# Mixture-of-experts weights in another slot order, with whole transfers and rows spread by a repeated column

## The reference

```python
def _hier_moe(h, w_group, b_group, w_expert, b_expert, w_gate, w_up, w_down):
    ...                                   # top-1 group, top-2 of its 8 experts, combine weights
    for g in range(N_GROUPS):             # 4 groups of 8 experts
        a = jnp.einsum('td,edf->tef', t, w_gate[g])
        u = jnp.einsum('td,edf->tef', t, w_up[g])
        act = jax.nn.silu(a) * u * combine[:, g, :, None]
        y = y + jnp.einsum('tef,efd->td', act, w_down[g])

def reference(x, p, ...):
    for i in range(DEPTH):                # 2
        x = x + mixer(_rmsnorm(x, norm_mix[i]), ...)
        x = x + _hier_moe(_rmsnorm(x, norm_ffn[i]), ...)
        gate = jax.nn.sigmoid(_rmsnorm(x, norm_ple[i]) @ ple_w_gate[i])
        x = x + gate * (p[i] @ ple_w_proj[i])
    return x
```

## Time and profile before

| | us |
|---|---|
| median of 3 executions | 842.86 (839.48, 842.86, 842.89) |
| the profiled execution's own time | 839.04 |
| its span, first to last instruction | 837.3 |
| PE busy | 750.0 (90%) |
| DVE, ACT, POOL busy | 377.8, 229.5, 189.8 |
| HBM read | 241.07 MB |

### The profile page before, as it was taken

The page is one execution under the profiler, slowest core; times in us unless marked ns, Lnnn a source line. Parts: engine busy times, 40 slices in busy tenths (PEclk is TensorE's granted clock), DMA queues, the critical chain, the costliest instruction groups (busy, mean ns, idle before and its releaser), DMA issues.

```text
span 837.3 us, 10837 instructions
## 1 busy us (share of the span) xinstructions
PE 750.0 (90%) x4121; PEld 413.0 (49%) x4121; DVE 377.8 (45%) x672; ACT 229.5 (27%) x416; POOL 189.8 (23%) x206
## 2 busy tenths in 40 slices
PE   2677879899999999889999977898999999989897
PEld 1555844643334333334778866456343343433366
DVE  6996842532222232213776968225332233222264
ACT  3323121431111110103675537143001111110163
POOL 5874420321111011000426560012210111100000
PEclk8598979999999999999999999999999999999999
DMA  7036061799999999999489572582899999999861
GB/s 227 1 58 203 2 237 70 282 413 412 412 413 413 412 416 411 413 415 370 175 253 280 206 287 66 205 286 113 306 412 413 412 413 413 412 416 411 344 228 50
DMA packets 79636, 244.48 MB, mean 292 GB/s; under 512 B 22080, under 2 KB 23120, under 8 KB 71008
## 3 DMA queue, kind: packets, MB, share of 16 engines
q1 hardware_dynamic: 75392, 240.24, 74.6%
q0 software_dynamic: 1408, 3.24, 1.8%
q10 hardware_dynamic: 2784, 0.30, 0.3%
HBM read 241.07 MB, written 1.64 MB: 290 GB/s over the span
## 4 chain that ended last, share of the span: by engine, by line
PE 81%; DVE 7%; issue 5%; ACT 3%; DMA 1%; POOL 1%; SPq 1%; ACTq 0%; DVEq 0%
PE PS L1833 27%; PE PS L1863 13%; PE PS L1579 11%; PE PS L1873 7%; PE PS L2053 3%; PE PS L1761 3%; PE PS L1703 2%; PE PS L1637 2%; PE PS L1802 2%; PE PS L1957 2%; PE PS L1844 1%; POOL qrs L717 1%; PE PS L1718 1%; ACT prob L1000 1%; PE PS L1663 1%
## 5 line engine op out<-in xcount | busy, mean ns | idle before, releaser
L1833 PE MATMUL PS<-ring,xe 128*64 128x512 f32 x1024 | 228.0, 594 | 17.4 <-issue 15.0
L1833 PEld LDWEIGHTS PS<-ring,xe 128*64 128x64 f32 x1024 | 76.9, 137 | 163.6 <-issue 163.6
L1863 PE MATMUL PS<-ring,actT 128*64 128x512 f32 x512 | 116.9, 598 | 1.7 <-DVE actT L1341 1.4
L632 POOL COPY xe<-xg 128x512 f32 x60 | 47.6, 793 | 296.8 <-PE PS L1833 276.3
L1355 DVE TENSOR_TENSOR olo<-PS,ohi 128x512 fp32r<-128x512 f32 x64 | 44.2, 691 | 123.3 <-ACT ohi L892 123.3
L1341 DVE COPY actT<-PS 128x256 f32<-128x256 f32 x32 | 13.6, 424 | 173.1 <-PE PS L1844 173.1
L892 ACT ACTIVATE ohi<-PS 128x512 fp32r<-128x512 f32 x64 | 38.2, 597 | 153.1 <-PE PS L1863 153.1
L1046 DVE SCALAR_TENSOR_TENSOR ringr<-ring,gT,dwh 128x512 fp32r<-128x512 f32 x80 | 63.6, 846 | 25.9 <-ACT dwh L763 24.6
L884 ACT ACTIVATE act<-PS 128x256 f32<-128x256 f32 x32 | 12.3, 383 | 223.8 <-PE PS L1833 223.8
L1863 PEld LDWEIGHTS PS<-ring,actT 128*64 128x64 f32 x512 | 34.7, 136 | 67.2 <-issue 67.2
L1579 PE MATMUL PS<-ringr,rawh 128*128 128x512 f32 x160 | 63.4, 396 | 0.8 <-DVE ringr L1046 0.8
(11 more groups left out here) (321 smaller groups left out, 970.6 us busy)
## 6 DMA issues: line engine op xcount, KB each, us to landing
ring<-in_moe_w_gate SPq DMA_DIRECT2D x128, 512.0 KB, 16.5
ring<-in_moe_w_up SPq DMA_DIRECT2D x128, 512.0 KB, 17.3
ring<-in_moe_w_down SPq DMA_DIRECT2D x64, 1024.0 KB, 17.4
ring<-in_nat_w_qkv SPq DMA_DIRECT2D x6, 2048.0 KB
ring<-in_ple_w_gate SPq DMA_DIRECT2D x4, 2048.0 KB
ring<-in_s_w_out SPq DMA_DIRECT2D x2, 2048.0 KB
ring<-in_nat_w_o SPq DMA_DIRECT2D x2, 2048.0 KB
ring<-in_s_w_in SPq DMA_DIRECT2D x1, 2048.0 KB
```

Source lines behind the costliest of these rows:

```text
L632: pool.tensor_copy(xe[:, e % 4, :, :], xg[:, :, bass.ds(first, CAP)]).then_inc(S("xe_ready"), 1)
L1833: ins = mm(PS[CAP * h_:CAP * h_ + CAP, 0, :].rearrange("p (u f) -> p u f", u=2), xe[:, (2 * p + h_) % 4, k, :], wv[h_][:, k], start=k == 0 ...
L1863: ins = mm(PS[CAP * h_:CAP * h_ + CAP, 2 + n, :], actT[:, k, CAP * h_:CAP * h_ + CAP], wd[h_][:, k, 512 * n:512 * n + 512], start=k == 0, ...
```

## The change

**Slots.** In layer 0 experts 2 and 3 of each six now have slots 4 and 5, experts 4 and 5 slots 0 and 1. `ys`, `yT[4]` and `glu` of the mixer moved out of slots 4 and 5, and the wait on `x_ready` is gone, so four experts' loads stand behind `y_done` where two did. The PLE's three items of layer 0 moved from slots 0, 1, 2 to 2, 3, 0. QKV, W_o and layer 1 are turned by two slots, which keeps what each of them waits for.

**Transfers.** The first six experts and pairs 5 to 15 ask for gate and up whole, 8 KB a partition, after `gu_done` alone; only pairs 3 and 4 come in halves. Where a pair came whole, PE waits for all of it before its first half.

**Rows.** `diag`, `rows` and `spread_rows` are gone. `spread_row` takes the column `slot` (or `wgt`) repeated 128 times as the stationary operand, against the identity: 4 matmuls of 128x128 each. The slots' row comes ahead of `gather`, the weights' row after its fourth k. `sel` is made and used one token half at a time for k = 0 and 1. POOL no longer waits for `row_done`. `wrow` is copied out when `gather` is through.

**Last combine.** `combine` of pair 15 stands ahead of the wait for `pj`, where it stood behind.

```diff
-        moe_items(0, (2, 3, 0, 1, 4, 5))
-        IT["ple"] = [ple_items(0, 0)]
+        moe_items(0, (2, 3, 4, 5, 0, 1))
+        IT["ple"] = [ple_items(0, 2)]
...
-        moe_items(1, (3, 0, 4, 5, 1, 2))
-        IT["ple"].append(ple_items(1, 1))
+        moe_items(1, (1, 2, 4, 5, 3, 0))
+        IT["ple"].append(ple_items(1, 3))
...
+        IN_HALVES = (3, 4)
+
+        def in_halves(n):
+
+            return (n - moe_item[0 if n < moe_item[1] else 1]) // 2 in IN_HALVES
...
-                for half, sem in enumerate((loaded[s], later[s])):
-                    cs = slice(1024 * half, 1024 * half + 1024)
-                    sp.dma_start(ring[s][:, 0:2048][:, cs], gate_[1][:, cs]).then_inc(sem, 16 if half else 64)
-                    sp.dma_start(ring[s][:, 2048:4096][:, cs], up_[1][:, cs]).then_inc(sem, 16)
+                sp.dma_start(ring[s][:, 0:2048], gate_[1]).then_inc(loaded[s], 80)
+                sp.dma_start(ring[s][:, 2048:4096], up_[1]).then_inc(later[s], 32)
...
+                if not in_halves(n):
+                    sp.wait_ge(S("gu_done"), NP * i + e // 2 - 2)
+                    for m in (n, n + 1):
+                        s, (gate_, up_, down_) = items[m]
+                        sp.dma_start(ring[s][:, 0:2048], gate_[1]).then_inc(loaded[s], 80)
+                        sp.dma_start(ring[s][:, 2048:4096], up_[1]).then_inc(later[s], 32)
+                    return
...
+            def gather_part(i, k, t):
+                for w, half in enumerate((hhi, hlo)):
+                    ins = mm(PS[:, GBANK[k], :], half[:, t, k, :], sel[:, t, :], start=(w, t) == (0, 0),
+                             stop=(w, t) == (1, 1))
+                return ins
...
+            def spread_row(i, n, what):
+
+                for j in range(2):
                     for t in range(TT):
-                        ins = mm(PS[:, GBANK[k], :], half[:, t, k, :], sel[:, t, :], start=(w, t) == (0, 0),
-                                 stop=(w, t) == (1, 1))
-                ins.then_inc(S("gather_done"), 1)
-
-            def spread_rows(i):
-
-                for n in range(2):
-                    pe.wait_ge(S("xg_ready"), KD * i + n + 3)
-                    pe.wait_ge(S("diag_ready"), 2 * TT * i + TT * n + TT)
-                    mm(PS[:, 2 + n, :], ones[:, :].bitcast(F32), diag[:, n].rearrange("p j t s -> p (j t s)"), start=True, stop=True)\
-                        .then_inc(S("row_done"), 1)
+                        ins = mm(PS[:, 4 + n, T * j + P * t:T * j + P * t + P], bc(what[:, t, j], 1, P), ident[:, :],
+                                 start=True, stop=True)
+                ins.then_inc(S("row_done"), 1)
...
                     if k0 == 0:
                         arrived(pe, it)
-                    else:
+                    if k0 or not in_halves(it):
                         later_arrived(pe, it)
...
                 down(i, NP - 1, 0)
                 down(i, NP - 1, 1)
+                combine(i, NP - 1)
                 pj = IT["ple"][i][1]
...
-                combine(i, NP - 1)
```

More of the change, by code:

```diff
@@ L194, in ple_items @@
             return (a, b, c)
-        moe_items(0, (2, 3, 0, 1, 4, 5))
-        IT["ple"] = [ple_items(0, 0)]
+        moe_items(0, (2, 3, 4, 5, 0, 1))
+        IT["ple"] = [ple_items(0, 2)]
         wq = I["nat_w_qkv"][0].rearrange("(k p) n -> p k n", p=P)
-        IT["qkv"] = [item((3 + n) % 4, (0, wq[:, :, 512 * n:512 * n + 512])) for n in range(6)]
+        IT["qkv"] = [item((1 + n) % 4, (0, wq[:, :, 512 * n:512 * n + 512])) for n in range(6)]
         wo = I["nat_w_o"][0].rearrange("(k p) n -> p k n", p=P)
-        IT["wo"] = [item((1 + n) % 4, (0, wo[:, :, 512 * n:512 * n + 512])) for n in range(2)]
-        moe_items(1, (3, 0, 4, 5, 1, 2))
-        IT["ple"].append(ple_items(1, 1))
+        IT["wo"] = [item((3 + n) % 4, (0, wo[:, :, 512 * n:512 * n + 512])) for n in range(2)]
+        moe_items(1, (1, 2, 4, 5, 3, 0))
+        IT["ple"].append(ple_items(1, 3))
         prev, nth, last, cnt = [], [], {}, {}
@@ L297, in program @@
               enumerate((A_R + 16384, A_R + 20480, A_O, A_O + 4096, A_H + 12288, O1 + 20480))]
-        ys = at("ys", [P, L, 8, SH], F32, A_XG + 24576)
-        yT = [at(f"yT{n}", [P, SW // P, T], F32, A_XG + 4096 * n) for n in range(5)]
-        glu = [at(f"glu{n}", [P, 512], F32, A_XG + 20480 + 2048 * n) for n in range(2)]
+        ys = at("ys", [P, L, 8, SH], F32, A_H + 8192)
+        yT = [at(f"yT{n}", [P, SW // P, T], F32, A_H + 4096 if n == 4 else A_XG + 4096 * n) for n in range(5)]
+        glu = [at(f"glu{n}", [P, 512], F32, A_O + 2048 * n) for n in range(2)]
         RX = A_W
@@ L519, in _ @@
                 for e in range(6):
-                    if items[m0 + e][0] == 4:
-                        if i == 0:
-                            sp.wait_ge(S("x_ready"), 1)
-                        else:
-                            sp.wait_ge(S("pv_done"), NPR)
+                    if i == 1 and items[m0 + e][0] == 4:
+                        sp.wait_ge(S("pv_done"), NPR)
                     load_gate_up(m0 + e)
@@ L1272, in route @@
                         bc(PS[:, 4, 0:TT * NE].rearrange("p (t e) -> p t e", t=TT), 2, 2), ALU.mult))
-                link(ve.tensor_reduce(slot[:, :, :].rearrange("p t j -> p (t j)"),
-                                      ptmp[:, :, :, :].rearrange("p t j e -> p (t j) e"), AX.X, ALU.add))
+                ve.tensor_reduce(slot[:, :, :].rearrange("p t j -> p (t j)"),
+                                 ptmp[:, :, :, :].rearrange("p t j e -> p (t j) e"), AX.X, ALU.add)\
+                    .then_inc(S("route_steps"), 1)
+                ve.wait_ge(S("route_steps"), 3 * i + 1)
                 ve.wait_ge(S("wr_ready"), 2 * i + 2)
                 for t in range(TT):
-                    ins = ts(sel[:, t, :], iota_s[:, :], slot[:, t, 0:1], None, ALU.is_equal)
-                link(ins)
-                for t in range(TT):
+                    link(ts(sel[:, t, :], iota_s[:, :], slot[:, t, 0:1], None, ALU.is_equal))
                     stt(sel[:, t, :], iota_s[:, :], slot[:, t, 1:2], sel[:, t, :].bitcast(F32), ALU.is_equal,
@@ L1300, in bounds_of, with weights_row @@
                 link(ts(col[:, :], col[:, :], -1.0, None, ALU.add))
[L1302 to L1308, removed]
+            def weights_row(i):
                 ve.wait_ge(S("gex_ready"), i + 1)
@@ L1311, in rows @@
                 link(ve.reciprocal(wgt[:, :, 0], den[:, :]))
[L1312 to L1315, removed]
+                tt(wgt[:, :, 1], e21[:, :], wgt[:, :, 0], ALU.mult).then_inc(S("route_steps"), 1)
             def rows_evict(i):
@@ L1361, in moe @@
                 route(i)
+                weights_row(i)
                 bounds_of(i)
-                rows(i)
                 rows_evict(i)
@@ L1884, in moe @@
                 places(i)
-                constant(5)
+                constant(4)
+                pe.wait_ge(S("route_steps"), 3 * i + 1)
+                spread_row(i, 0, slot)
                 pe.wait_ge(S("hhi_ready"), TT * (i + 1))
                 pe.wait_ge(S("hlo_ready"), TT * (i + 1))
-                pe.wait_ge(S("sel_ready"), TT * (i + 1))
                 pe.wait_ge(x_part[i], 4)
-                for k in range(KD):
+                for t in range(TT):
+                    pe.wait_ge(S("sel_ready"), TT * i + t + 1)
+                    for k in range(2):
+                        ins = gather_part(i, k, t)
+                        if t:
+                            ins.then_inc(S("gather_done"), 1)
+                for k in range(2, KD):
                     gather(i, k)
+                    if k == 3:
+                        pe.wait_ge(S("route_steps"), 3 * i + 2)
+                        pe.wait_ge(S("route_steps"), 3 * i + 3)
+                        spread_row(i, 1, wgt)
                 for p in range(NP):
                     gate_up(i, p, 0, 4)
-                    if p == 0:
-                        spread_rows(i)
                     gate_up(i, p, 4, KD)
```

13 lines of the change are left out of this document (7 added, 6 removed).

## The result

| | us |
|---|---|
| kernel before, median of 12 in this comparison | 840.52 (835.41 to 842.89) |
| changed kernel, median of 12 | 843.81 (841.86 to 849.00) |
| ratio, 95% interval | 1.0056 [1.0035, 1.0078] |
| profiled execution, before and after | 839.04, 843.37 |
| its span | 837.3, 841.6 |

By the ratio the change makes the kernel slower by 0.56%, 4.7 us, just past the half per cent that can be told; the interval begins at 0.35%, and the two medians lie 3.3 us apart. The prediction had 843.0 with 834 to 849 around it, and called that no change against a median before of 842.86.

A forecast was written before the change was run, and what follows sets the result against it. Landing of pair 15's gate and up was taken to bound each layer's experts, then PE from dense_mm. Layer 0 +4.4 and layer 1 -1.5 gave +2.9 on 839.0, 841.9; the median was put at 843.0 us, range 834 to 849.

The forecast's parts named there:

- The forecast of no change: Whole kernel: a median of 843.0 against 842.86 before; chance 0.48 of staying within 0.5%, 4.2 us.
- Early loads, -1.7: Layer 0's stream: four experts loaded early bring pair 15's second half from 374.6 to 372.9 us, -1.7; nothing in layer 1.
- Rows, end of pair 0: Both layers: pair 0 ends 2.2 us sooner and starts 0.2 sooner; the stream gains 2.0 of 2.9, -2.2 a layer.
- Whole transfers, -3.5 and +3.4: Pairs 5 to 15, both layers: 422 instead of 409 GB/s, -3.5; pair 15 takes 7.04 us after its last byte, +3.4.
- Clock falls, +0.8 before pair 15: PE in both layers: a fall to 1.2 GHz costs 1.7 us, half counted; layer 1's gather gains 0.8.
- Last down product in layer 0: 387.2 forecast: End of pair 15's down product in layer 0: 387.2 us instead of 390.4, 3.2 earlier.
- The late PLE weights, 18.6 us behind it: PLE of layer 0: pj waits for pair 15, dense_mm starts 18.6 us behind the down product against 11.0, +7.6.
- Layer 1's combine, +0.8: Layer 1's PLE: the last combine runs ahead of the transposes and copy of p, +0.8 us.
- The stream wins: Rival: whole transfers at 430 GB/s, thin queue cured, no clock falls; -7.1 us, 834 to 836; chance 0.27.
- PE in the cold at the PLE: Rival: low clock at layer 0's PLE and pair 15s, thin queue uncured; +11.2 at worst, likely 849 us; chance 0.25.
- The early loads do nothing: Rival: something else holds layer 0's stream, so the 1.7 us are missing; 844.7 us; chance 0.05.
- three things that would have made me wrong: Signs against the forecast: ga landing before 396, the stream exceeding 425 GB/s, or PE waiting for pairs 5 to 10.

The follow-up runs named there:

- experiment 8: The kernel before with the early loads of layer 0 alone; 841.69 us, 1.0007 to the kernel before.
- experiment 2: The kernel before with only the dense blocks' slots turned as in the change, so PLE weights wait for pair 15; 847.24 us, 1.0094.
- experiment 10: The changed kernel with 8 constant matmuls between the halves of pair 0 in both layers; 847.25 us, 1.0097 to the kernel before.
- experiment 7: The kernel before with the new rows and selection alone; 838.10 us, 0.9976 to the kernel before.
- experiments 3: The changed kernel with every pair from 3 to 15 in halves; 843.15 us, 1.0041 to the kernel before.
- experiment 4: The changed kernel with pair 15 in halves besides 3 and 4; 841.33 us, 1.0022 to the kernel before.
- experiments 1: The changed kernel with the dense blocks' old slots, so PLE weights wait for pair 14; 838.68 us, 0.9983 to the kernel before.
- experiment 9: The changed kernel with PLE weights behind pair 14, pairs 11 to 15 also in halves, last combine behind the transposes of p; 830.72 us, 0.9885.
- experiment 12: The version of experiment 9 with pairs 3 and 4 whole too; 833.42 us, 0.9920 to the kernel before.

## Why the prediction was right in sum and wrong in a step

**The forecast of no change.** Measured +0.56%. The sum, +2.9 on 839.04, was near; the 1.1 us that took 841.9 to 843.0 were added because the three executions of the kernel before had a median of 842.86. Over twelve executions that median is 840.52, so as a difference the forecast said +0.1 where +3.3 was measured by the medians and 4.7 by the ratio. That 843.0 lies so near 843.81 is in part luck.

**Early loads, -1.7.** Right in mechanism and size, -1.6 by the trace of experiment 8; no median shows it alone. It gave layer 0's gather, with the same idle gap as layer 1's, no price for the clock that it lost in experiments 2 and 8.

**Rows, end of pair 0.** PE's part came: pair 0 to pair 1 is 2.08 us shorter, by 2.2 in the step, and each row's 4 matmuls take 1.05 us for 1.0. What failed is "With pair 0 and pair 1 over 2.2 us sooner I take 2.0 of the 2.9". By experiment 10 it is 1.0 to 1.25 in a layer, by experiment 7 1.3 in layer 1 and nothing in layer 0. I had read the thin stretch in layer 1's window and applied it to layer 0, where the queue was still full at pair 0's end; it becomes thin there only through the early loads, so the two parts pay together: from pair 0's start to pair 15's second half the early loads save 1.6 us without the new rows and 3.3 with them (200.22 in experiment 7, 196.95 in 3, whose first six experts come whole too). The change itself shows the stretch still thin, 303 GB/s from 593 to 603. "There the queue is nearly empty" was not a reading either: the DMA engines were busy for 0.98 of the stretch at 354 GB/s, and are for 0.92 here. Why they move less while busy is open. Pair 3's 4.19 MB, 10 us of data, are asked for at 591.27 and 594.71, and pair 4's first half follows at 599.52.

**Whole transfers, -3.5 and +3.4.** Measured -2.9 by landing (experiments 3 and the change) and +3.4; the rate went from 413 to 421, not 422. A layer is 0.5 worse for it by the traces, and all halves were 0.7 us better in all, by medians that can't be told apart. The Trainium skill (DMA: Bandwidth & Descriptors, Anatomy of one DMA) has 2.0 us of fixed cost in a transfer; its fit is for single transfers issued by GpSimd, and these are issued by SP into a full queue. Here 44 fewer transfers a layer, with rows twice as long, gave 2.9 us in all, 0.07 each, so that cost is not paid for each transfer in this queue, as the prediction had said.

**Clock falls, +0.8 before pair 15.** The place was wrong. The fall came at pair 14 in both layers, and the wait for pair 15's data covered all of it. It counts as soon as the data are early, as experiment 4 shows. In layer 1 the gather gained 1.5 us, where I took 0.8 with 0.2 of the start.

**Last down product in layer 0: 387.2 forecast, 388.7 measured.** Against `glu_done`, which was itself 0.9 later, the forecast is 0.6 off: the data 1.4 later than its -7.4 (a thin queue worth less, whole transfers worth less), the clock 0.8 better.

**The late PLE weights, 18.6 us behind it.** Measured 17.3: p lands 5.9 us after its issue (7.0 by the earlier trace rows), `ga` 11.2 (12.4), and the low clock costs 5.33 - 3.70 = 1.6 where I took 1.7. `dense_mm` was forecast at 405.8 and starts at 406.00. This step carried the forecast, and experiments 1 and 2 bear it out.

**Layer 1's combine, +0.8.** Measured +0.8 (from the last down product's end to `dense_mm` 11.3 before, 12.1 after), 1.1 by experiment 9.

**The sum.** Layer 0 +4.4 forecast, +3.7 measured; layer 1 -1.5 and -0.7. The other 1.3 us lie in the two mixers, which the sum doesn't touch. Of the 0.9 before `glu_done`, the clock from 125 to 150 was 0.97 instead of 1.00. It was 0.94 to 1.00 in the runs with early loads and 0.97 in experiment 2, which has none and reached `glu_done` at 151.61, so the early loads need have no part in it. By its traces the change costs +3.0 where the sum said +2.9; errors of a microsecond went both ways in it.

**The rivals.** "The stream wins" fell with 421 GB/s, under the 430 from which it decides. "PE in the cold at the PLE" came in one part, the low clock at the projections; at 17.3 us it stayed under its 20. "The early loads do nothing" has the median of experiment 8 for it and the trace, -1.6 behind pair 0's start, against it. None of the three things that would have made me wrong was seen: `ga` landed at 399.9, the stream stays at 421, and PE first waits for pair 11.

## What to carry to other kernels

Where a weight's slot comes free sets when it can be asked for; before turning a list of slots, follow the first load behind the stream to the event that frees its slot, since two places in a list cost 5 us here, more than all the rest gave. The last unit of a stream that waits for data should come in pieces, whatever suits the units before it. A step on one engine is worth only what the queue behind it can use at that moment, so the window that prices it must be taken in every layer in which it is claimed.

## What the runs showed of the hardware

In experiment 12, where all transfers at the start of the stream are whole, ten microseconds in each layer ran at 428 GB/s, more than the 421 of the long stretch, and the whole transfers of layer 1's first experts in experiment 10 reached 433:

```profile
186.00:196.00 10.00, 9.28 (x44) 3.54 (x42) 3.40 (x8) 1.58 (x3) 1.59 (x2) 1.00 1.01 428
...
593.00:603.00 10.00, 9.28 (x44) 3.52 (x42) 3.61 (x8) 1.58 (x3) 1.58 (x2) 1.00 1.02 428
```

```profile
540.00:550.00 10.00, 10.00 (x24) 4.39 (x24) 0.69 (x1) 0.00 (x0) 0.00 (x0) 1.00 1.03 433
```

No ten microseconds of these traces were read above that. The Trainium skill (DMA: Bandwidth & Descriptors, Where 436 GB/s comes from) has the ceiling at 435; over ten microseconds the traces agree with it as a ceiling. What holds the long stretch at 421 was not tried.

An idle gap of about 2 us ahead of one long `gate_up` was followed by the 1.2 GHz level in some executions (8.78 us instead of 7.09), at pair 12, 13 or 14, and not behind equal gaps at other pairs; the same waiting cut in two, 0.65 and 1.45 us, was never followed by it in any trace here. And the same gap of 1.8 us before the gather left the clock alone in layer 0 of the kernel before and not in experiments 2 and 8.
